# The second block's token mixer rewritten: keys first, value and gate slabs inside the levels of the inverse, norms as one scalar per token, output with tokens on partitions, masks on GpSimd

## What is computed

```python
b_qkv = jax.nn.silu(causal_dwconv_2(b_qkv, conv_w))            # 4 taps, per channel
q = q * lax.rsqrt(jnp.sum(q * q, -1, keepdims=True) + 1e-6) * (dk ** -0.5)
k = k * lax.rsqrt(jnp.sum(k * k, -1, keepdims=True) + 1e-6)
gc = jnp.cumsum(...)                                           # log decay, per head
decay = jnp.exp(jnp.where(lower, gc[..., :, None] - gc[..., None, :], -jnp.inf))
m = jnp.where(strict, jnp.einsum('bhnid,bhnjd->bhnij', k_beta, kc) * decay, 0.0)
sol = lax.linalg.triangular_solve(eye + m, rhs, left_side=True, lower=True, unit_diagonal=True)
attn_local = jnp.einsum('bhnid,bhnjd->bhnij', qc, kc) * decay
# scan over chunks: v_new = u - w S;  o = q_dec S + attn_local v_new;  S = gl S + k_dec^T v_new
o = o * lax.rsqrt(jnp.mean(o * o, -1, keepdims=True) + 1e-6) * norm_g
o = o * jax.nn.silu(z)
mix = jnp.concatenate([y_a, y_b, y_c], axis=-1) @ w_out
```

## Time and profile before

| | us |
|---|---|
| median of 3 runs | 3282.94 (3281.27 to 3284.68) |
| profiled execution, its own time | 3278.74 |
| span of the profiled execution | 3276.9 |
| TensorE busy | 3053.5 (93%) |
| VectorE busy | 2035.7 (62%) |
| ScalarE busy | 1619.0 (49%) |
| GpSimd busy | 0.6 (0%) |

### The profile page before, as it was taken

How to read it: one execution, slowest core, us unless ns; L and a number is a source line. 1 busy time by engine, 2 the same in 40 slices (tenths; PEclk the granted TensorE clock), 3 DMA queues, 4 the chain that set the end, 5 groups by cost and what they waited for, 6 DMA issues and landing times.

```text
span 3276.9 us, 41014 instructions
## 1 busy us (share of the span) xinstructions
PE 3053.5 (93%) x16672; PEld 2615.1 (80%) x16672; DVE 2035.7 (62%) x2116; ACT 1619.0 (49%) x1720; POOL 0.6 (0%) x8
## 2 busy tenths in 40 slices
PE   6989999999989999997879987879999999999997
PEld 5879997877879997876767877768878888888886
DVE  4456665545446665557765577655585567547988
ACT  4446654444446654445424453334464455446775
POOL 0000000000000000000000000000000000000000
PEclk9999999999999999998999998989999999999999
DMA  5534445544544444543224532044586568557995
GB/s 201 193 135 159 147 168 177 192 171 153 184 145 154 144 176 172 186 161 129 88 84 178 183 130 91 27 180 180 199 305 241 176 248 303 185 181 294 360 348 216
DMA packets 84849, 601.24 MB, mean 183 GB/s; under 512 B 9408, under 2 KB 10176, under 8 KB 13120
## 3 DMA queue, kind: packets, MB, share of 16 engines
q1 hardware_dynamic: 80928, 586.75, 49.0%
q10 hardware_dynamic: 3744, 11.95, 1.0%
HBM read 597.61 MB, written 1.05 MB: 183 GB/s over the span
## 4 chain that ended last, share of the span: by engine, by line
PE 84%; DVE 10%; ACT 3%; issue 2%; DMA 1%; ACTq 0%; DVEq 0%; SPq 0%
PE actb L502 48%; PE acc L502 22%; PE dveb L502 11%; DVE wl L1773 2%; ACT wh L1177 2%; PE dveb L588 1%; DVE mix L2054 1%; PE dveb L620 1%; PE dveb L663 1%; DVE mix L2485 0%; DVE mix L2369 0%; DVE x L1818 0%; DVE ht L1832 0%; PE acc L782 0%; DVE mix_r L1996 0%
## 5 line engine op out<-in xcount | busy, mean ns | idle before, releaser
L1773 DVE TENSOR_TENSOR wl<-raw,wh 128x2048 fp32r<-128x2048 f32 x407 | 931.6, 2291 | 654.0 <-ACT wh L1177 651.3
L502 PE MATMUL actb<-wh,x 128*128 128x512 f32 (+1 forms) x3760 | 1091.5, 371 | 11.3 <-DVE wl L1773 11.3
L1177 ACT ACTIVATE wh<-raw 128x2048 fp32r<-128x2048 f32 x407 | 777.7, 1913 | 556.4 <-PE acc L502 287.6
L502 PEld LDWEIGHTS actb<-wh,x 128*128 128x128 f32 x3760 | 688.5, 190 | 134.4 <-DVE wl L1773 11.9
L502 PE MATMUL acc<-wh,x2m 128*128 128x512 f32 x2104 | 691.0, 399 | 14.6 <-DVE wl L1773 7.4
L502 PE MATMUL actb<-wl,x 128*128 128x512 f32 (+1 forms) x1880 | 694.8, 370 | 0.0
L502 PEld LDWEIGHTS acc<-wh,x2m 128*128 128x128 f32 x2104 | 397.7, 189 | 98.1 <-issue 15.2
L1773 DVE TENSOR_TENSOR wl<-mix,wh 128x2048 fp32r<-128x2048 f32 x150 | 343.8, 2292 | 175.5 <-ACT wh L1177 172.2
L502 PE MATMUL acc<-wl,x2m 128*128 128x512 f32 x1052 | 412.1, 392 | 0.0
L502 PEld LDWEIGHTS actb<-wl,x 128*128 128x128 f32 x1880 | 357.3, 190 | 59.3 <-issue 0.5
L1177 ACT ACTIVATE wh<-mix 128x2048 fp32r<-128x2048 f32 x150 | 287.5, 1916 | 176.1 <-PE acc L502 90.5
(11 more groups left out here) (360 smaller groups left out, 2785.1 us busy)
## 6 DMA issues: line engine op xcount, KB each, us to landing
raw<-stream SPq DMA_DIRECT2D x293, 1024.0 KB, 4.8
mix<-experts SPq DMA_DIRECT2D x150, 1024.0 KB, 4.8
raw<-experts SPq DMA_DIRECT2D x114, 1024.0 KB, 4.8
gain<-rows_w ACTq DMA_DIRECT2D x16, 512.0 KB, 4.2
mix<-const ACTq DMA_DIRECT2D x1, 1216.0 KB, 5.5
ht<-x_t SPq DMA_DIRECT2D x1, 1024.0 KB, 4.8
mix<-gmlp_w ACTq DMA_DIRECT2D x2, 512.0 KB, 4.9
out<-ht SPq DMA_DIRECT2D x2, 512.0 KB, 2.6
```

The lines of the kernel that those rows point to most:

```text
L502: return pe.matmul(out, lhs, rhs, start=start, stop=stop, skip_group_check=True)
L1177: go(wh[:, d * SLAB:(d + 1) * SLAB], raw_at(m), ACT.Copy).then_inc(S["hi_done"], c.one("hi_done"))
L1773: TT(wl[:, d:d + SLAB], raw_at(m), asf(wh[:, d:d + SLAB]), ALU.subtract).then_inc(S["lo_done"], c.one("lo_done"))
```

## The change

The stream order becomes k, k, cq, ck, cv, q, q, then inside the levels av, v, v, au, z and in the tail the second z. The keys come first, so the matrix can be built before the q and v slabs arrive. The convolution's first tap moves to ScalarE (`tap`, a copy with a per-channel scale), the three others stay on VectorE (`conv_rest`). q and k are no longer normalised: sums of squares are column matmuls with one result column per head and chunk (`sums`), a Sqrt and a RECIPROCAL of 128x8 give one scalar per token (`rkc`), and the scalars are folded into `MT` and `AT` (`decayed`), the key decay, the state's weights, and by a small transposed row into beta. The scale of q cancels in the output norm except for epsilon (`qsc`). The gate rows are spread in halves and copied out by ScalarE. VectorE does its work on the current level before it splits the next slab (`take` and a later `ahead`). GpSimd makes all the masked `MLT` of levels 1 to 6, one level ahead. The output is made with tokens on partitions, so its norm is one scalar per token and head; it is turned by TensorE, and the output slabs are spread through the tail.

The stream, and GpSimd's part:

```diff
 def layer2_stream(l):
-    s = cols("w_in_2", (l,), QKV1, 6)
-    for first in (CQ1, CK1, CV1, AV1, AU1, Z1, Z1 + WIDE):
+    q, k, v = (QKV1 + 2 * WIDE * j for j in range(3))
+    s = []
+    for first in (k, k + WIDE, CQ1, CK1, CV1, q, q + WIDE, AV1, v, v + WIDE, AU1, Z1, Z1 + WIDE):
...
+                pool.wait_ge(S["mt_ready"], l + 1)
+                for level in range(1, 7):
+                    if level > 1:
+                        pool.wait_ge(S["y_ready"], 12 * l + 2 * (level - 1))
+                    for ch in range(2):
+                        o = slice(ch * 512, (ch + 1) * 512)
+                        nc.gpsimd.tensor_tensor(MLT[:, o].rearrange("p (h t) -> p h t", h=4),
+                                                MT[:, o].rearrange("p (h t) -> p h t", h=4),
+                                                t2("level", level * P, P).unsqueeze(1).to_broadcast([P, 4, P]),
+                                                ALU.mult).then_inc(S["ml_ready"], 1)
```

TensorE inside the levels:

```diff
+                    if level == 2:
+                        project_into(acc[:, 2, :])
+                        pe.wait_ge(S["sq_ready"], c.next("sq_ready", 2))
+                        sums(acc[:, 3, :], qsq).then_inc(S["qsum_full"], 1)
+                    if level == 3:
+                        pe.wait_ge(S["qs_ready"], c.next("qs_ready"))
+                        project_into(acc[:, 3, :])
+                        c.add(("frees", "conv_done"), 2)
+                        block_scores(1)
+                    if level == 4:
+                        pe.wait_ge(S["qk_ready"], c.next("qk_ready", 2))
+                        products(0, 0)
+                        products(0, 1)
                         project("act", "gelu_ready", x2v, tokens=True)
...
+                        turn_probs(0, 1, "att", "aT_full")
+                        project("act", "silz_ready", x2v, tokens=True)
```

The tap on ScalarE, and on VectorE the scalars in place of wide norms (keys and matrix, then the output):

```diff
+                def tap(n, j, t, bank):
+
+                    act.wait_ge(S["slab_used"], c.at("slab_used", n + 1))
+                    for f in range(2):
+                        last = go(cacc2[:, t * 512 + f * T:t * 512 + (f + 1) * T], bank[:, f * T:(f + 1) * T], ACT.Copy,
+                                  scale=prm("conv_w_2", l, 36 + 2 * j + f))
...
-                    V.reciprocal(XT[:, 0:512], s).then_inc(S["std_taken"], c.one("std_taken"))
...
+                    for h in range(4):
+                        o = (4 * ch + h) * P
+                        last = STT(dst[:, o:o + P], b[:, h * P:(h + 1) * P], rkc[:, 4 * ch + h:4 * ch + h + 1], DT[:, o:o + P],
+                                   ALU.mult, ALU.mult)
...
+                V.reciprocal(rkc, rkc).then_inc(S["rk_ready"], c.one("rk_ready"))
...
-                    V.reciprocal(r, r).then_inc(S["dve_step"], c.one("dve_step"))
...
+                    step(V.tensor_reduce(osq[:, o4], g4(c8(sqo, ch)), AX.X, ALU.add))
...
+                    step(V.reciprocal(osc[:, o4], osq[:, o4]))
+                    for h in range(4):
+                        o = (4 * ch + h) * P
+                        last = STT(OT[:, o:o + P], dveb[:, ch, h * P:(h + 1) * P], osc[:, 4 * ch + h:4 * ch + h + 1],
+                                   silz[:, o:o + P], ALU.mult, ALU.mult)
```

More of the change, by code:

```diff
@@ new lines, in broadcast, with sums @@
+                def broadcast(bank, pair, first):
+                    for j in range(2):
+                        m = mm(bank[:, j * T:(j + 1) * T], pick_row(4, 2 * pair + j), rows2[0:4, first:first + T], True, True)
+                    return m
+                def sums(bank, src):
+                    for h in range(4):
+                        for ch in range(2):
+                            m = mm(bank[:, 4 * ch + h:4 * ch + h + 1], at_chunk(src[h // 2], h % 2, ch), ones[:, 0:1], True, True)
+                    return m
@@ new lines, in layer2 @@
+                first = c.get("dve_unit")
+                assert first % 2 == 0 and c.get("act_unit") % 2 == 0
+                small_weights(unit("dve", "dve_free"))
+                project("dve", "conv_done")
+                project("dve", "conv_done")
+                pe.wait_ge(S["rows_ready"], c.next("rows_ready"))
+                bank = unit("act", "col_ready")
+                for ch in range(2):
+                    for part in range(2):
+                        last = pe.transpose(bank[:, (2 * ch + part) * 4:(2 * ch + part + 1) * 4],
+                                            rows2[0:4, part * T + ch * P:part * T + (ch + 1) * P], c1("ident", 4, 0, 4))
@@ new lines, in take, with conv_silu @@
+                def take():
+                    return c.slab()
+                def tap(n, j, t, bank):
+                    act.wait_ge(S["slab_used"], c.at("slab_used", n + 1))
+                    for f in range(2):
+                        last = go(cacc2[:, t * 512 + f * T:t * 512 + (f + 1) * T], bank[:, f * T:(f + 1) * T], ACT.Copy,
+                                  scale=prm("conv_w_2", l, 36 + 2 * j + f))
+                    last.then_inc(S["tap_ready"], c.one("tap_ready"))
+                def conv_silu(j, t, sq=None):
+                    act.wait_ge(S["conv_done"], c.next("conv_done"))
+                    d = qkvc[:, j * 512:(j + 1) * 512]
+                    go(d, cacc2[:, t * 512:(t + 1) * 512], ACT.Silu).then_inc(S["qk_ready"], c.one("qk_ready"))
+                    if sq is not None:
+                        act.wait_ge(S["qk_ready"], c.own("qk_ready"))
+                        go(sq, d, ACT.Square).then_inc(S["sq_ready"], c.one("sq_ready"))
@@ L1663, in exps, with spread, ys @@
+                def spread(part, pair, bank):
+                    go(BC.rearrange("p (h w t) -> p h w t", h=4, w=2)[:, 2 * pair:2 * pair + 2, part, :],
+                       bank.rearrange("p (h t) -> p h t", h=2), ACT.Copy).then_inc(S["bc_ready"], c.one("bc_ready"))
+                def ys():
+                    for ch in range(2):
+                        go(Y[:, ch * 512:(ch + 1) * 512], bank_in(), ACT.Copy).then_inc(S["y_ready"], c.one("y_ready"))
                 def exps(i):
@@ L1684, in layer2 @@
+                for ch in range(2):
+                    go(X[:, ch * 512:(ch + 1) * 512], bank_in(), ACT.Copy).then_inc(S["x_first"], c.one("x_first"))
+                n = None
                 for level in range(1, 7):
[L1685 to L1688 removed]
+                    ys()
+                    if level < 6:
+                        n = take()
+                        ahead(n + 2)
@@ L2493, in layer2 @@
-                for j in range(4):
-                    slab()
+                n = take()
+                out_lo(0)
+                ahead(n + 2)
+                n = take()
+                out_norm(1)
+                ahead(n + 2)
+                n = take()
+                out_lo(1)
+                ahead(n + 2)
                 layer_norm()
```

571 lines of the change are left out of this document (305 added, 266 removed).

## The result

The changed kernel takes 3254.89 us (median of 4 runs, 3253.01 to 3255.49) beside 3283.52 for the kernel before: ratio 0.9912, 95% interval 0.9897 to 0.9927. It is 28.6 us faster; the forecast was 53.4. Its profiled execution took 3254.55.

The account below looks back on a forecast made before the run. VectorE's 9.7 us between projections was taken to bound the first part, a cross-engine chain the levels. First mixer 27.1 - 1.9 - 1.2 = 24.0, second 29.4, sum 53.4: 3225.3 profiled, 3229.5 as median; range 3210 to 3258.

Parts of the forecast that it names:

- the likeliest case: Whole kernel: the forecast sum of 53.4 us gained holds, giving 3229.5 us; chance 0.51.
- a port that lengthens the levels: Levels: GpSimd masks and VectorE's two-input `wl` stop each other, 26 us back, 3256; chance 0.15.
- a late ScalarE: First parts: ScalarE's single queue holds each of seven slabs for 1.9 us, 13 of 27 lost per mixer, 3256; chance 0.12.
- the 0.17 left out: Whole kernel: the chance the prediction gave to times outside its range of 3210 to 3258.
- the signs: New trace: first part 60 to 64 us, levels 85 to 93 led by products, 24 masks of 1 to 2, first tail 38 to 41.
- one sign of being wrong: New trace: VectorE rows beside a GpSimd mask being longer than alone would show the prediction wrong.
- The last rival: First part: TensorE at half clock, not VectorE, holds it; gain under 10 per mixer, 3265; chance 0.04.
- the 27.1: First part of the mixer: forecast gain in us, level 1 starting at 60.6 and not at 87.7.
- My late times: Levels 2 to 5: us by which VectorE's late work was forecast to delay the subtractions, 2.2, 3.3, 1.7 and 0.4.
- The first rival: Levels of both mixers: GpSimd masks and VectorE's `wl` contend for a shared port, 26 us back, 3256; chance 0.15.
- my slower rival: Levels: GpSimd masks too long, TensorE waiting for them; at 7.7 us per mask the gain is gone; chance 0.05.
- clock and levels: Levels and first part: VectorE never late, 7.6 more per mixer, 3214, and fuller clock in the first part; chance 0.13.

Follow-up runs that it names:

- e3: Changed kernel with the split of the router's small weights moved from level 3 of the last mixer to behind level 6; 3248.08 us.
- e4: Changed kernel with three extra groups of unused products added in TensorE's wait in level 3 of both mixers; 3247.48 us.
- e7: Changed kernel with four unused 128x512 reciprocals put back on VectorE in each first part, behind the key and query convolutions; 3266.01 us.
- e11: Changed kernel with several order edits combined, plus the first mixer's tail rounding its last slab behind the norm instead of ahead; 3216.46 us.
- e2: Changed kernel with TensorE issuing the second block's scores ahead of the slab in level 3, not behind it; 3243.10 us.
- e8: Changed kernel with VectorE's level 2 order made statistics, scores, `wl`, then the gated branch's norm; 3247.40 us.
- e1: Changed kernel with the next slab's rounding requested ahead of the second mixer's gate functions (ScalarE) and gate rows (VectorE); 3250.04 us.
- e12: Kernel before the change with only its level masks moved to GpSimd; 3280.34 us, ratio 0.9993.
- e6: Changed kernel with every level mask computed three times over on GpSimd; 3283.51 us, ratio 1.0000 to the kernel before.

## Why the prediction was right, and where a size was off

The time fell in the range (3210 to 3258) but outside the likeliest case's own (3218 to 3242). That it is in the range owes something to luck: the range went up to 3258 for the sake of two rivals at 3256, a port that lengthens the levels and a late ScalarE, and neither is what cost the 25. (The cases inside the range have 0.91 together, so the 0.17 left out do not follow from the list.) The mechanisms were right in the main; four sizes were not.

Of the signs, GpSimd's 24 masks of 1.28 to 1.78, the first tail (39.2) and the second mixer's norm beside products came as said, and no mask released TensorE. The first parts (65.3 and 71.7 for 60 to 64) and the second mixer's levels (95.7 for 85 to 93) did not. Levels 2 to 4 are led by `wl` and not by products, which the prediction's own late times already implied. And one sign of being wrong did come: VectorE's rows beside a mask are longer than alone, here where nothing waits for them.

*First part.* TensorE's waits went as said: 2.55 for the gate rows (forecast 2.4) and 1.03 for the copy (1.2). The mis-sized term is TensorE's: I priced slabs and products at full clock, 56.7, and they took 61.73, 3.3 of it behind the wait for the scanned rows. The other 1.7, in the last slab, follow no wait of TensorE's; their cause stays open. In e3, e4, e7 and e11 the first part is 2.6 to 2.8 shorter. The last rival named this term; it costs 5.0 per mixer and is not the bound. And "VectorE bound it by its reciprocals" is only half true: e7 shows the keys' two hidden in the new order, and 11.5 of the 27.1 are two slabs that left the first part.

*Levels.* My late times were 2.2, 3.3, 1.7 and 0.4; the waits are 2.55, 3.73, 1.57 and 0.88. What failed is that I added each wait once. The one of 3.73 costs 3.5 more in half clock (2.8 to 3.7 by e4), and the first mixer's levels are 3.3 over my sum. e2 and e8 show that order alone made these waits: level 2 from 16.7 to 14.2, level 3 from 19.1 to 13.7.

*The second mixer.* I took its first part and its levels for the first's. Two things of its own were not in the sum: its second slab is not rounded when it starts (5.6, e1), since the change put that rounding behind the gate functions; and the split of the router's weights stands ahead of `wl` in level 3 (3.3, e3). Together 8.9 of its 16.9.

*The start.* 4.7 of the shortfall lie ahead of the first mixer. It is scatter of the execution: ahead of the mixer the same 12 products take 4.37 and not 2.85, in a stretch (1450 to 1475) with a clock of 0.86 and not 0.93; the changed kernel's two profiles differ by 2.4, and e12, whose program up to there is that of the kernel before (1498.4), starts it at 1502.3. A forecast can't know it; it belongs to the range.

*Masks.* A mask costs 1.28 and is hidden; a level goes on 0.05 us after its last subtraction, where it was 0.82. The first rival's price (26 us) did not come, since in this order the masks of the levels fall on convolutions from PSUM, which they leave alone, on VectorE's idle time, or on a `wl` that TensorE does not wait for. But e6 and e12 show the mechanism is real, and that my slower rival was wrong in its size: it took masks for too long from 7.7 us on, while three masks of 1.28 already eat the whole gain. Its rule counted only TensorE's waits for masks; the price came from VectorE's instructions that the masks lengthen (gated norm, probabilities, `wl`).

*Tail.* 39.2 and 43.3 against 39.7 and 44.1. That the first mixer's norm waits for the last `wh` was said; e11 shows it was 7.4 for nothing.

*Rivals.* The late queue of ScalarE held one slab of the second mixer (5.5) and not seven in each; clock and levels came out worse, not better.

## What to carry to other kernels

Price a long wait of TensorE twice, once for itself and once for the clock behind it (here 3.73 and some 3), and look first for an order that removes it; filling it with idle products won as well (2.8 to 3.7). When work moves off an engine that covered something, walk every instance of the stage: here the second mixer's uncovered slab and its extra split cost 8.9 of 29.3 us. Work put on GpSimd was free here where VectorE read from PSUM, idled, or was not waited for; elsewhere it lengthened VectorE's instructions. Taking the masks off GpSimd cost 14.6 us in one order (12.9 of them by the place that level 1's pair got), and putting them on it won no more than 2.6 in another.

## What the runs showed of the hardware

Waits of the same length were not followed by the same clock: 2.55 in level 2 cost nothing in the changed kernel (clock 1.00 behind it), the same 2.55 in the second mixer of e1 was followed by 8.03 us at 0.57, and 2.55 at the scan by 10.23 us at 0.68. The wait of 3.73 in level 3 was followed by less than full clock in every trace that has it (0.50 or 0.59 over 8.3 us). What sets this was not tried. A GpSimd product of two 128x512 operands takes 1.28 us; beside VectorE's instructions with two SBUF operands either of them lasts longer (1.71 for 0.69, 2.86 for 2.29, 3.35 for 1.28). Six of VectorE's taps, which read one tensor from PSUM and one from SBUF, keep their 2.67; two TENSOR_SCALAR with one tensor from SBUF to SBUF do not (1.85 for 0.73, e6).
